# Two transformer blocks on one core: low parts of the weights by accumulating DMAs in the first feed-forward

## The chip, the cores and the metric

The kernel runs on one core of one Trainium2 chip. The metric is the device time of one execution in microseconds. A core has TensorE (PE, matmuls into PSUM), VectorE (DVE), ScalarE (ACT), GpSimd (POOL) and SyncE (SP); SP, ACT and POOL issue DMAs. Each engine works through its own queue in order, and they are tied together by semaphores.

## The reference

Two hybrid transformer blocks follow each other on 16 meta tokens and 512 tokens of width 1024, in float32. The first mixes a short convolution, retention and differential attention and ends in a feed-forward; the second mixes stick-breaking attention and gated linear attention and has a gated feed-forward. What the change touches is the feed-forward of the first block:

```
D_MODEL = 1024
D_FF = 4 * D_MODEL
...
    x = x + merged @ w_out

    u = jnp.square(jax.nn.relu(rms_norm(x, norm2_w) @ w_up))
    return x + u @ w_down
```

## The kernel before

**Products in three passes.** All activations lie with their features on the 128 partitions and the tokens along the free axis. Every product with a weight is done as three products of rounded operands: a float32 value is split into a high part, rounded to the matmul's type `fp32r`, and a low part, the difference. A product is high x high, high weight x low activation, and low weight x high activation. The high and low parts of the activations lie in `xh`, `xl` and `bh`, `bl`.

**Strips.** The weights come from HBM as 331 strips of 128 x 8 x 128 values (512 KB), 128 output columns each. There are two buffers for the raw strip (`wraw`), for its high part (`wh`) and for its low part (`wl`), used in turn: `slot` is the strip's number modulo 2. For a strip n:

- SP loads it (`load`, L366) when the low part of strip n-2 is made (`lo_done`), which is the last reader of that raw buffer.
- ACT rounds it: `split_hi` (L401 to L406) waits for the load and until strip n-2 is multiplied (`mm_done`), and writes `wh`, which counts `hi_done`.
- DVE subtracts: `split_lo` (L972 to L976) waits for `hi_done` and writes `wl = wraw - wh`, which counts `lo_done`.
- PE multiplies: `strip` (L1776 to L1801) waits for `hi_done` and for the eviction of strip n-2, does 8 matmuls of the pass high x high and 8 of high x low, waits for `lo_done`, and does 8 of low x high; the last one counts `mm_done`. A strip with `ready` (the first of each phase whose input is being made) instead waits for `lo_done` at once and goes by chunks of the input, three matmuls each.

**The first feed-forward.** Its 4096 hidden features are done in four groups of 1024. A group is 8 up strips (`ffn0up` to `ffn3up`, source `bh`, `bl`) and 8 down strips (`ffn0down` to `ffn3down`, source `xh`, `xl`), 64 strips in all, for 512 tokens.

- In an up strip n, ACT (`up_strips`, L663 to L673) first does `split_hi` of strip n+1, waits for the matmuls of n, writes relu of the sum to `tmp` (L671), waits for DVE's `u_scaled`, and rounds the result to `xh` (`hi_of`, L414). DVE (L1341 to L1359) does, through `begin` (L978), `split_lo` of strip n+1 and waits for the matmuls of n; it then squares by relu(sum) x `tmp` (L1348, which frees the PSUM bank), multiplies by the norm's row `rsq` (L1354), and makes `xl` after `xh` (L985).
- In a down strip, ACT only does `split_hi` (`splits`, L487). DVE's `accumulate` (L1324 to L1331) does `begin` and adds the sum to `res`. The last down group goes through `finished_rows` instead, with norms of the next block in between.
- GpSimd has loaded the attention tables before (L2429) and built the masks (L2431 to L2447); its next work is a loop of subtractions for gated linear attention (L2450 on), much later.

The order on each queue is the program's order: what stands in the loop body is what each engine does next.

Of the kernel before, what the change touches and what calls it, by code (L numbers as in the profile page):

```python
# [23 lines left out]
ALU = mybir.AluOpType  # L24
ACT = mybir.ActivationFunctionType
# [4 lines left out]
KC = D // P  # L30
# [37 lines left out]
START = {}  # L68
# [47 lines left out]
def build(nc, weights, cols, tables, consts, lam_rows, post_rows, x_t, meta2_t, wgk, gla_masks, res_dram,  # L116
          mrg_dram, out):
    ctx = ExitStack()
    with ctx:
# [3 lines left out]
        def sem(name):  # L123
            return ctx.enter_context(nc.semaphore(name))
# [89 lines left out]

        w_loaded = [sem("w_loaded0"), sem("w_loaded1")]
        hi_done, lo_done = sem("hi_done"), sem("lo_done")
        mm_done = sem("mm_done")
        evicted = [sem("evicted0"), sem("evicted1")]
        in_ready, op_ready = sem("in_ready"), sem("op_ready")
# [171 lines left out]
        def _(act):  # L391
# [9 lines left out]
            def split_hi(n, half, slot):  # L401

                act.wait_ge(w_loaded[slot], 16 * half + 16)
                if not (isinstance(n, int) and n < 2):
                    act.wait_ge(mm_done, n - 1)
                nc.scalar.activation(wh[:, slot], wraw[:, slot], ACT.Copy).then_inc(hi_done, 1)  # L406

            def begin(n_half_slot, next_one):

# [77 lines left out]
            def splits(B, count):  # L487

                with act.Fori(0, count // 2) as i:
                    for j in range(2):  # L490
                        split_hi(*pos(B, j + 1, i))
# [168 lines left out]
            for g in range(4):  # L660
                B = START[f"ffn{g}up"]

                def up_strips(i):  # L663
                    for j in range(2):
                        p0, p1 = pos(B, j, i), pos(B, j + 1, i)
                        split_hi(*p1)
                        if g == 0 and isinstance(i, int) and j == 0:
                            act.wait_ge(sums_done, 2)
                            root(rsq[:, NM:T], ps[:, 4, :], 1.0 / D, -1.0)
                        act.wait_ge(mm_done, p0[0] + 1)  # L670
                        nc.scalar.activation(tmp[:, j, NM:T], slot_ap(p0[2], SEQ), ACT.Relu).then_inc(relu_ready, 1)  # L671
                        act.wait_ge(u_scaled, KC * g + 2 * i + j + 1)
                        hi_of(flat(xh[:, bass.ds(2 * i + j, 1), NM:T]), hf[:, j, NM:T])  # L673

                first_then_loop(act, KC // 2, up_strips)
                n_hi += KC
                if g < 3:
                    splits(START[f"ffn{g}down"], KC)
                if g == 2:
                    act.wait_ge(meta_in, 16)  # L680
                    nc.scalar.activation(msq.rearrange("p (c t) -> p c t", c=KC), res[:, :, 0:NM], ACT.Square)
                    act.wait_ge(meta_scaled, 1)
                    nc.scalar.activation(bh[:, :, 0:NM], mscaled.rearrange("p (c t) -> p c t", c=KC), ACT.Copy)\
                        .then_inc(meta_hi, 1)
# [282 lines left out]
        def _(dve):  # L967
# [4 lines left out]
            def split_lo(n, half, slot):  # L972

                dve.wait_ge(hi_done, n + 1)
                nc.vector.tensor_tensor(wl[:, slot], wraw[:, slot], wh[:, slot].bitcast(F32), ALU.subtract)\  # L975
                    .then_inc(lo_done, 1)  # L976

            def begin(this, next_one):  # L978
                split_lo(*next_one)
                dve.wait_ge(mm_done, this[0] + 1)  # L980

            def lo_of(dst, src, hi, ready, n):
# [341 lines left out]
            def accumulate(B, n=SEQ):  # L1324

                with dve.Fori(0, KC // 2) as i:
                    for j in range(2):
                        p0 = pos(B, j, i)
                        begin(p0, pos(B, j + 1, i))
                        r = flat(res[:, bass.ds(2 * i + j, 1), T - n:T])  # L1330
                        nc.vector.tensor_tensor(r, slot_ap(p0[2], n), r, ALU.add).then_inc(evicted[p0[2]], 1)  # L1331

# [5 lines left out]
            for g in range(4):  # L1338
                B = START[f"ffn{g}up"]

                def up_strips(i):  # L1341
                    for j in range(2):
                        p0 = pos(B, j, i)
                        begin(p0, pos(B, j + 1, i))
                        dve.wait_ge(relu_ready, KC * g + 2 * i + j + 1)
                        dve.wait_ge(op_ready, (3 + g) * KC + 2 * i + j - 1)

                        nc.vector.scalar_tensor_tensor(out=hf[:, j, NM:T], in0=slot_ap(p0[2], SEQ), scalar=0.0,  # L1348
                                                       in1=tmp[:, j, NM:T], op0=ALU.max, op1=ALU.mult)\
                            .then_inc(evicted[p0[2]], 1)  # L1350
                        if g == 0 and isinstance(i, int) and j == 0:
                            root_made()
                        dve.wait_ge(evicted[p0[2]], p0[1] + 1)
                        nc.vector.tensor_tensor(hf[:, j, NM:T], hf[:, j, NM:T], rsq[:, NM:T], ALU.mult)\  # L1354
                            .then_inc(u_scaled, 1)
                        dve.wait_ge(u_scaled, KC * g + 2 * i + j + 1)
                        c = bass.ds(2 * i + j, 1)
                        lo_of(flat(xl[:, c, NM:T]), hf[:, j, NM:T], flat(xh[:, c, NM:T]), op_ready,
                              n_hi + 2 * i + j + 1)  # L1359

                first_then_loop(dve, KC // 2, up_strips)
                n_hi += KC
                if g < 3:
                    accumulate(START[f"ffn{g}down"])
                if g == 2:
                    dve.wait_ge(meta_in, 16)
                    m3 = mscaled.rearrange("p (c t) -> p c t", c=KC)
                    nc.vector.tensor_tensor(m3, res[:, :, 0:NM],
                                            wcols("norm_mix_pre_2").unsqueeze(2).to_broadcast([P, KC, NM]), ALU.mult)\
                        .then_inc(meta_scaled, 1)  # L1370
                    dve.wait_ge(meta_hi, 1)
                    link(nc.vector.tensor_tensor(bl[:, :, 0:NM], m3, bh[:, :, 0:NM].bitcast(F32), ALU.subtract))
# [1045 lines left out]
        @block.gpsimd  # L2418
        def _(pool):
            for h in range(RH + DH):  # L2420
                if h == 0:
                    pool.wait_ge(op_ready, KC)
                elif h == RH:
                    pool.wait_ge(op_ready, 2 * KC)
                elif 1 < h < RH:
                    pool.wait_ge(rs_masked, 5 * (h - 1))
                elif h > RH + 1:
                    pool.wait_ge(ds_ready, 3 * (h - RH - 1))
                pool.dma_start(tbl[h % 2], tables[h]).then_inc(table_in[h % 2], 16)  # L2429

            nc.gpsimd.memset(sbmask[:], 0.0).then_inc(pool_self, 1)  # L2431

            def masked_where(lo, hi, base, step, per_partition, op):

                masked_where.n += 1
                pool.wait_ge(pool_self, masked_where.n)
                m = sbmask[:, lo:hi]
                nc.gpsimd.affine_select(out=m, in_=m, compare_op=op, fill=-1e30, base=base, pattern=[[step, hi - lo]],
                                        channel_multiplier=per_partition).then_inc(pool_self, 1)

            masked_where.n = 0
            for lo, hi, base in ((0, P, 0), (272, 400, 0), (416, 432, 112), (432, 448, 0)):
                masked_where(lo, hi, base, 1, -1, ALU.is_gt)
            masked_where(416, 432, -111, 0, 1, ALU.is_gt)
            pool.wait_ge(const_in, 16)
            pool.wait_ge(pool_self, 6)
            nc.gpsimd.tensor_copy(identb[:], ident).then_inc(masks_made, 1)  # L2447


            for h in range(GH):  # L2450
                pool.wait_ge(gcum_done, 2 * h + 1)
                for k, L, lo in levels():
                    m = 7 * h + k
                    if m >= 2:
                        pool.wait_ge(gx_ready, m - 1)
                    d, s_ = halves(grow[m % 2], L, lo), halves(cums[h % 2], L, lo)
                    n = (T - lo) // (2 * L)
                    mid = s_[:, :, 0, L - 1:L].to_broadcast([P, n, L])
                    nc.gpsimd.tensor_tensor(d[:, :, 0, :], mid, s_[:, :, 0, :], ALU.subtract)
                    nc.gpsimd.tensor_tensor(d[:, :, 1, :], s_[:, :, 1, :], mid, ALU.subtract).then_inc(gd_ready, 1)  # L2460
# [130 lines left out]
```

## Time and profile before

| | us |
|---|---|
| median of three runs | 2198.74 (2198.53 to 2198.84) |
| span of the profiled execution | 2196.6 |
| PE busy | 2150.5 (98%) |
| DVE busy | 1150.0 (52%) |
| ACT busy | 776.6 (35%) |
| POOL busy | 51.3 (2%) |

How to read it: busy times are added up by engine; a share of the span is a mean over stages with different limits. Times of instructions are counted from the start of the profiled span. Where several instructions of one kind follow each other, a line shows them together with their count. "L1797" is a line of the kernel's file; that of a helper stands for all its callers, and the names of tiles tell them apart. Matmuls overlap, so their durations are longer than their distance.

### The profile page before, as it was taken

The page shows a single profiled execution, that of the slowest core. Times are in us where ns is not written, and L with a number is a line of the kernel's source. Part 1 is how long each engine was busy: PE and PEld are TensorE (multiplying, and loading weights), DVE is VectorE, ACT ScalarE, POOL GpSimd, SP SyncE. Part 2 cuts the span into 40 slices and gives each one's busy share as a digit, 9 for nine tenths or more (in the row PEclk, how much of TensorE's full clock was granted, in tenths as well). Part 3 has the DMA queues.
Part 4 walks back from the last instruction along what each step waited for, and adds up shares of the span by engine and source line. Part 5 has one row for each costly group of instructions (what it writes and reads, how often), then busy time and mean ns, then how long its engine had stood idle before and what let it go on. Part 6 is the DMA issues. An engine that isn't in the chain of part 4 may idle for free.

```text
span 2196.6 us, 33725 instructions
## 1 busy us (share of the span) xinstructions
PE 2150.5 (98%) x13184; PEld 1851.5 (84%) x13184; DVE 1150.0 (52%) x1719; ACT 776.6 (35%) x1214; POOL 51.3 (2%) x79
## 2 busy tenths in 40 slices
PE   9999998999999999999999999999999989999998
PEld 8988994677888778888888888999999988889896
DVE  6553332443555645535445665457755556546365
ACT  4222221332344533323223466333433333222233
POOL 0000000000000000000000000012200000000000
PEclk9999999999999999999999999999999999999999
DMA  4232220132222132223222221231123222222222
GB/s 148 93 105 95 86 86 20 58 106 95 74 72 68 58 126 96 92 96 101 90 96 95 83 92 58 86 118 59 54 103 128 94 77 77 95 87 96 96 87 96
DMA packets 52966, 194.66 MB, mean 89 GB/s; under 512 B 6896, under 2 KB 7280, under 8 KB 52224
## 3 DMA queue, kind: packets, MB, share of 16 engines
q1 hardware_dynamic: 49248, 177.56, 24.6%
q10 hardware_dynamic: 2656, 12.41, 1.5%
q0 software_dynamic: 960, 3.24, 0.5%
q8 instruction: 75, 1.23, 0.2%
q14 instruction: 27, 0.22, 0.0%
HBM read 186.77 MB, written 6.42 MB: 88 GB/s over the span
## 4 chain that ended last, share of the span: by engine, by line
PE 93%; DVE 4%; ACT 2%; issue 1%; DMA 0%; DVEq 0%; ACTq 0%; SPq 0%
PE ps L1797 75%; PE ps L2356 5%; PE ps L2223 1%; PE ps L2013 1%; PE ps L2038 1%; PE ps L1972 1%; PE ps L1957 1%; PE ps L2288 1%; PE ps L2129 1%; DVE kk_r L1441 1%; PE ps L2052 1%; ACT kk L715 0%; ACT kk L716 0%; PE ps L2266 0%; PE ps L2110 0%
## 5 line engine op out<-in xcount | busy, mean ns | idle before, releaser
L406 ACT ACTIVATE wh<-wraw 128x1024 fp32r<-128x1024 f32 x330 | 348.2, 1055 | 834.4 <-PE ps L1797 725.5
L975 DVE TENSOR_TENSOR wl<-wraw,wh 128x1024 fp32r<-128x1024 f32 x330 | 403.4, 1223 | 144.9 <-ACT wh L406 138.0
L1797 PE MATMUL ps<-xh,wh 128*128 128x264 f32 (+1 forms) x2088 | 392.2, 333 | 9.7 <-ACT wh L406 5.7
L1797 PE MATMUL ps<-xh,wl 128*128 128x264 f32 (+1 forms) x2088 | 385.9, 330 | 0.0
L1797 PE MATMUL ps<-xl,wh 128*128 128x264 f32 (+1 forms) x2088 | 385.8, 330 | 0.0
L1797 PEld LDWEIGHTS ps<-xh,wh 128*128 128x128 f32 x2088 | 315.9, 189 | 51.8 <-ACT wh L406 4.6
L1797 PEld LDWEIGHTS ps<-xh,wl 128*128 128x128 f32 x2088 | 316.3, 188 | 38.2
L1797 PEld LDWEIGHTS ps<-xl,wh 128*128 128x128 f32 x2088 | 316.3, 188 | 38.2
L1797 PE MATMUL ps<-bh,wh 128*128 128x264 f32 (+1 forms) x1296 | 234.3, 325 | 3.9 <-DVE hf L1008 1.7
L1797 PE MATMUL ps<-bl,wh 128*128 128x264 f32 (+1 forms) x1296 | 230.9, 322 | 0.0
L1797 PE MATMUL ps<-bh,wl 128*128 128x264 f32 (+1 forms) x1296 | 230.6, 322 | 0.0
L1797 PEld LDWEIGHTS ps<-bh,wh 128*128 128x128 f32 x1296 | 191.4, 188 | 27.1 <-DVE hf L1008 2.2
L1797 PEld LDWEIGHTS ps<-bl,wh 128*128 128x128 f32 x1296 | 191.3, 188 | 19.8 <-issue 0.2
L1797 PEld LDWEIGHTS ps<-bh,wl 128*128 128x128 f32 x1296 | 191.0, 188 | 19.6
L1008 DVE TENSOR_TENSOR qq<-ps,rsq 128x528 f32<-128x528 f32 (+2 forms) x36 | 25.3, 704 | 80.6 <-PE ps L1797 80.5
L414 ACT ACTIVATE bh<-hf 128x512 f32 (+1 forms) x38 | 24.0, 632 | 103.3 <-DVE hf L1697 52.3
L1008 DVE TENSOR_TENSOR tmp<-ps,rsq 128x528 f32<-128x528 f32 x31 | 21.9, 708 | 64.9 <-PE ps L1797 63.3
L1331 DVE TENSOR_TENSOR res<-ps,res 128x512 f32 x24 | 16.6, 692 | 72.5 <-PE ps L1797 72.5
L2356 PE MATMUL ps<-wh,bh 128*128 128x512 f32 x176 | 49.1, 393 | 0.0
L2356 PE MATMUL ps<-wh,bl 128*128 128x512 f32 x176 | 49.0, 393 | 0.0
L2356 PE MATMUL ps<-wl,bh 128*128 128x512 f32 x176 | 49.0, 393 | 0.0
L1008 DVE TENSOR_TENSOR gate<-ps,rsq 128x512 f32<-128x512 f32 (+1 forms) x24 | 16.7, 697 | 57.8 <-PE ps L1797 56.3
(420 smaller groups left out, 2030.1 us busy)
## 6 DMA issues: line engine op xcount, KB each, us to landing
wraw<-weights_dram SPq DMA_DIRECT2D x331, 512.0 KB, 3.5
hf<-tables_dram POOLq DMA_DIRECT2D x12, 264.0 KB, 3.0
res<-x_t_dram SPq DMA_DIRECT2D x4, 528.0 KB, 7.4
res<-x_t_dram ACTq DMA_DIRECT2D x1, 2112.0 KB, 9.1
res_dram<-res ACTq DMA_DIRECT2D x1, 2112.0 KB, 7.7
mrg_dram<-mrg ACTq DMA_DIRECT2D x1, 2112.0 KB, 7.3
mrg<-mrg_dram ACTq DMA_DIRECT2D x1, 2112.0 KB, 10.6
res<-res_dram ACTq DMA_DIRECT2D x1, 2112.0 KB, 16.5
```

The source lines that it names most:

```text
L406: nc.scalar.activation(wh[:, slot], wraw[:, slot], ACT.Copy).then_inc(hi_done, 1)
L414: nc.scalar.activation(dst, src, ACT.Copy, scale=scale).then_inc(hf_hi, 1)
L975: nc.vector.tensor_tensor(wl[:, slot], wraw[:, slot], wh[:, slot].bitcast(F32), ALU.subtract)\
L1008: return nc.vector.tensor_tensor(dst, src, row(rsq, n), ALU.mult)
L1441: ins = nc.vector.tensor_tensor(dst, src, hi.bitcast(F32), ALU.subtract)
L1797: last = nc.tensor.matmul(o, w[:, slot, c, :], a[:, c, tok], start=(k == 0), stop=(k == len(steps) - 1))
L1957: ins = nc.tensor.matmul(o, keys, qq[:, h, NM + q0:T], start=True, stop=True)
L1972: ins = nc.tensor.matmul(o, vt[:, t, f:f + P], at[:, t - 1, q0:SEQ], start=False, stop=(t == 4))
L2013: ins = nc.tensor.matmul(ps[:, 2 + m, off:off + W], dq[h % 2][f, NM + P * b:NM + P * b + P], dk[h % 2][f, 0:W], start=True, stop=True)
L2038: nc.tensor.matmul(ps[:, 6, q0:SEQ], vt[:, t, P * h:P * h + P], at[:, t, q0:SEQ], start=(t == 0), stop=False)
L2052: nc.tensor.transpose(ps[:, 4, P * k:P * k + P], a[:, keys:keys + P], ident)
L2356: last = nc.tensor.matmul(ps[:, 2 * t + h, :], a[:, c, NM + P * t:NM + P * t + P], w[:, slot, 4 * h:4 * h + 4, :].rearrange("p k n -> p (k ...
```

## The change

ACT, after it has rounded a strip to `wh`, writes the negative of the same rounding to `wl` (`split_minus_hi`) and counts `minus_hi`. GpSimd waits for each of these and issues a DMA from SBUF to SBUF that adds the raw strip onto `wl`, so that `wl = wraw - wh` stands there when it has landed; a semaphore for each slot counts it (`raw_added`). DVE no longer subtracts: `begin_added` waits for the landing of the next strip's DMA and counts `lo_done` by a nop, in the place where the subtraction stood. This is done for 56 strips in a row, from the second up strip of the first group to the first down strip of the last group. The first up strip of the first group and the last seven down strips keep the subtraction, as does all the rest of the kernel. SP's loads, PE's waits and the buffers stay as they are.

```diff
@@ -214,6 +214,7 @@
         w_loaded = [sem("w_loaded0"), sem("w_loaded1")]
         hi_done, lo_done = sem("hi_done"), sem("lo_done")
+        minus_hi, raw_added = sem("minus_hi"), [sem("raw_added0"), sem("raw_added1")]
         mm_done = sem("mm_done")
@@ -404,6 +405,11 @@
                 nc.scalar.activation(wh[:, slot], wraw[:, slot], ACT.Copy).then_inc(hi_done, 1)
+
+            def split_minus_hi(n, half, slot):
+
+                split_hi(n, half, slot)
+                nc.scalar.activation(wl[:, slot], wraw[:, slot], ACT.Copy, scale=-1.0).then_inc(minus_hi, 1)
 
@@ -663,7 +669,7 @@
                         p0, p1 = pos(B, j, i), pos(B, j + 1, i)
-                        split_hi(*p1)
+                        split_minus_hi(*p1)
@@ -675,7 +681,9 @@
                 if g < 3:
-                    splits(START[f"ffn{g}down"], KC)
+                    with act.Fori(0, KC // 2) as i:
+                        for j in range(2):
+                            split_minus_hi(*pos(START[f"ffn{g}down"], j + 1, i))
@@ -979,6 +987,15 @@
+            def begin_added(this, next_one):
+
+                _, half, slot = next_one
+                first = START["ffn0up"] + 1
+                done = half - (first + (slot != first % 2)) // 2 + 1
+                dve.wait_ge(raw_added[slot], 16 * done)
+                nc.vector.nop().then_inc(lo_done, 1)
+                dve.wait_ge(mm_done, this[0] + 1)
+
@@ -1326,7 +1343,7 @@
                         p0 = pos(B, j, i)
-                        begin(p0, pos(B, j + 1, i))
+                        begin_added(p0, pos(B, j + 1, i))
                         r = flat(res[:, bass.ds(2 * i + j, 1), T - n:T])
@@ -1341,7 +1358,7 @@
                         p0 = pos(B, j, i)
-                        begin(p0, pos(B, j + 1, i))
+                        begin_added(p0, pos(B, j + 1, i))
                         dve.wait_ge(relu_ready, KC * g + 2 * i + j + 1)
@@ -2446,6 +2463,12 @@
             nc.gpsimd.tensor_copy(identb[:], ident).then_inc(masks_made, 1)
 
+            first = START["ffn0up"] + 1
+            for k in range(56):
+                slot = (first + k) % 2
+                pool.wait_ge(minus_hi, k + 1)
+                pool.dma_start(wl[:, slot], wraw[:, slot], accum_op=ALU.add).then_inc(raw_added[slot], 16)
+
```

## Rows read from the trace of the kernel before

**Rows 1.** The page: busy time, share of the span and instructions of each engine.

```profile
PE 2150.5 (98%) x13184; PEld 1851.5 (84%) x13184; DVE 1150.0 (52%) x1719; ACT 776.6 (35%) x1214; POOL 51.3 (2%) x79
```

**Rows 2.** By stretches (us), TensorE alone: length, busy, granted clock, DMA share, GB/s.

```profile
892.00:1205.00 313.00, 313.00 (x1351) 1.00 0.29 94
...
1800.00:2196.00 396.00, 381.13 (x2148) 0.99 0.27 88
```

**Rows 3.** The chain that ended last, its piece in this stage: start, length, what.

```profile
892.74 317.46 PE ps L1797 x1370
```

**Rows 4.** In order of time: start, us, engine, line, operation; one up strip.

```profile
921.79 2.01 PE L1797 MATMUL ps<-bh,wh 128*128 128x512 f32 x8
...
922.71 0.69 DVE L1348 SCALAR_TENSOR_TENSOR hf<-ps,tmp 128x512 f32<-128x512 f32 x1 [1.16 <-ACT tmp L671]
923.44 0.69 DVE L1354 TENSOR_TENSOR hf<-hf,rsq 128x512 f32<-128x512 f32 x1
...
924.26 0.63 ACT L414 ACTIVATE xh<-hf 128x512 f32 x1 [1.67 <-DVE hf L1354]
924.80 1.04 ACT L406 ACTIVATE wh<-wraw 128x1024 fp32r<-128x1024 f32 x1
...
925.88 1.23 DVE L975 TENSOR_TENSOR wl<-wraw,wh 128x1024 fp32r<-128x1024 f32 x1
...
927.27 19.80 SPq L366 DMA_DIRECT2D wraw<-weights_dram  x5
927.35 2.01 PE L1797 MATMUL ps<-bh,wh 128*128 128x512 f32 x8
927.55 0.60 ACT L671 ACTIVATE tmp<-ps 128x512 f32<-128x512 f32 x1 [1.71 <-PE ps L1797]
928.27 0.69 DVE L1348 SCALAR_TENSOR_TENSOR hf<-ps,tmp 128x512 f32<-128x512 f32 x1 [1.17 <-ACT tmp L671]
```

**Rows 5.** Durations (ns, min/median/max) of both split lines, 890 to 1160 us.

```profile
L406 ACT ACTIVATE wh<-wraw x49: 1042/1049/1062, 890.4 to 1156.8; 128x1024 fp32r<-128x1024 f32 x49
...
L975 DVE TENSOR_TENSOR wl<-wraw,wh x49: 1224/1226/1227, 891.5 to 1158.0; 128x1024 fp32r<-128x1024 f32 x49
```

**Rows 6.** In order of time: two activations of ScalarE, one right behind the other.

```profile
882.24 1.06 ACT L406 ACTIVATE wh<-wraw 128x1024 fp32r<-128x1024 f32 x1 [3.37 <-PE ps L1797]
...
883.20 0.71 ACT L414 ACTIVATE bh<-res,col 128x512 fp32r<-128x512 f32 x1
```

**Rows 7.** The stage as one stretch: length, busy of PE, PEld, DVE, ACT, POOL; clock, DMA.

```profile
891.80:1204.00 312.20, 312.20 (x1347) 252.78 (x1346) 151.85 (x179) 96.95 (x124) 0.00 (x0) 1.00 0.29 94
```

**Rows 8.** In order of time: GpSimd's last mask and its next instruction.

```profile
710.59 0.55 POOL L2447 CAST identb<-cst 128x128 bf16<-128x128 f32 x1
1465.41 0.61 POOL L2459 TENSOR_TENSOR res<-res 128x256 f32<-128x256 f32 x1 [754.27 <-DVE res L1527]
```

**Rows 9.** The page, DMA issues: count, KB each, median us from issue to landing.

```profile
wraw<-weights_dram SPq DMA_DIRECT2D x331, 512.0 KB, 3.5
hf<-tables_dram POOLq DMA_DIRECT2D x12, 264.0 KB, 3.0
...
out_dram<-qq SPq DMA_DIRECT2D x7, 256.0 KB, 2.1
```

**Rows 10.** The page, DMA queues: packets, MB, share of 16 engines' span.

```profile
q1 hardware_dynamic: 49248, 177.56, 24.6%
...
q0 software_dynamic: 960, 3.24, 0.5%
```

**Rows 11.** Groups of eight strips as stretches (columns of rows 7), the second and third.

```profile
936.40:980.80 44.40, 44.40 (x193) 36.02 (x192) 17.04 (x18) 9.05 (x9) 0.00 (x0) 1.00 0.29 95
980.80:1025.30 44.50, 44.50 (x194) 36.10 (x193) 24.61 (x31) 16.79 (x24) 0.00 (x0) 1.00 0.29 94
```

**Rows 12.** In order of time: the first up strip of the first group begins.

```profile
887.54 0.40 PE L1797 MATMUL ps<-bh,wh 128*128 128x512 f32 x1
...
890.40 1.06 ACT L406 ACTIVATE wh<-wraw 128x1024 fp32r<-128x1024 f32 x1 [0.69 <-issue]
```

**Rows 13.** In order of time: a down strip on ScalarE and VectorE.

```profile
944.25 1.06 ACT L406 ACTIVATE wh<-wraw 128x1024 fp32r<-128x1024 f32 x1 [4.50 <-PE ps L1797]
944.38 0.69 DVE L1331 TENSOR_TENSOR res<-ps,res 128x512 f32 x1 [3.38 <-PE ps L1797]
945.35 1.23 DVE L975 TENSOR_TENSOR wl<-wraw,wh 128x1024 fp32r<-128x1024 f32 x1 [0.27 <-ACT wh L406]
```

**Rows 14.** The raw strips' loads, 900 to 1300 us: issue to landing.

```profile
DMA to landing us min/median/max: 3.2/3.4/4.5
```

**Rows 15.** By stretches (columns of rows 2): the end of the kernel.

```profile
2185.00:2190.00 5.00, 1.47 (x7) 1.00 0.55 203
2190.00:2196.00 6.00, 0.00 (x0) 0.54 0.47 175
```

## The prediction, made before the changed kernel was run

> **What bounds the kernel now.** I read the page first, then the stage of the first feed-forward by stretches, then the chain that ended last, and then one strip in order of time on every engine. The page gives TensorE 98% of the span, VectorE 52%, ScalarE 35% and GpSimd 2% [rows 1]. In the stretch from 892 to 1205 us TensorE is busy for 313.00 of 313.00 us, at a granted clock of 1.00, which is its upper level of 2.4 GHz [rows 2]. The chain that ended last runs through this stage in one piece of 317.46 us that is nothing but the matmuls of L1797 [rows 3]. So there is no idle time of TensorE here to be won back, and whatever is taken off VectorE in this stage is worth nothing by itself. The only question is whether something new becomes longer than TensorE's time for a strip.
>
> That time is the step from 921.79 to 927.35, 5.56 us for 24 matmuls [rows 4]; the stage has 64 such strips, and the change touches the low parts of 56 of them (1 to 56, counted from the first strip of ffn0up as 0).
>
> **The loop of an up strip, before.** The same rows show a loop beside TensorE, for a strip n: VectorE evicts n (L1348 at 922.71), scales it (923.44), ScalarE rounds it to xh (924.26) and then makes wh of strip n+2 (924.80), VectorE makes wl of n+2 (925.88, done 927.11), and only then may it evict n+1. Both queues are in order, so the eviction stands behind the weight's low part. From one eviction to the following wh is 924.80 - 922.71 = 2.09 us; from there to the end of wl 2.31 us. The loop takes about 4.5 us against 5.56, so it has 1.1 us to spare. This is the margin that the change spends.
>
> **Removed.** 56 subtractions of 1.226 us are 68.7 us of VectorE [rows 5]. TensorE waits for none of them: worth 0 us.
>
> **Added on ScalarE.** 56 negated roundings of the same shape as wh, 1.05 us each [rows 5], stand behind wh; a 128x1024 activation followed by another one is 0.96 us from start to start (882.24 to 883.20) [rows 6]. So the negated strip is complete 0.96 + 1.05 = 2.01 us after wh begins. The 59 us themselves fit, as ScalarE is busy for 96.95 of 312.20 us in this stage [rows 7]; what counts is where the 1.05 us lies, in the loop.
>
> **Added on GpSimd and the DMA queues.** GpSimd waits for minus_hi and issues a 512 KB accumulating transfer from SBUF to SBUF. Behind these waits on its queue stand only the subtractions of the later attention, which begin at 1465 us [rows 8]; they lose nothing. A queue takes about 0.16 us from the event to the issue, as SP does from wl (done 927.11) to its load (927.27) [rows 4]. No row shows an accumulating transfer, so I bound its time X from issue to landing. Lower end: GpSimd's plain 264 KB transfer lands in 3.0 us [rows 9]; its queue used 0.5% of 16 engines' span [rows 10], so 0.005 x 16 x 2196.6 / 12 / 16 = 0.92 us on each engine for one transfer, hence 1.77 us for 512 KB, and a plain 512 KB would land in 3.0 + 0.85 = 3.85 us. An accumulation must also read its destination: another 1.77 us gives 5.6 us, which I take, since reading twice is the least that adding needs. Upper end: the whole plain transfer twice, 7.7 us; I keep 9 us for the range, since nothing bounds the adding itself. The quickest large transfer of the whole trace, 256 KB from SBUF, takes 2.1 us [rows 9].
>
> The Trainium skill, "DMA: Bandwidth & Descriptors", section "Anatomy of one DMA", fits a transfer from GpSimd with 2.0 us plus its bytes at 436 GB/s, an estimate of 3.2 us for 512 KB; by it the sum below would end at about 2259 us. The trace's own 264 KB transfer, 3.0 us where this fit gives 2.6, speaks against so low a value, and the fit was made on plain copies.
>
> **The new wait.** begin_added makes VectorE wait for the landing of n+1 before it evicts n, with the operand's scaling and low part queued behind; ScalarE's xh waits for these, and wh and the negated copy of n+2 stand behind xh. So the DMA lies in the loop: 2.09 (eviction to wh) + 2.01 + 0.16 + X + 0.20 (landing to eviction with the nop between; I take 0.12 from the end of relu at 928.15 to the eviction at 928.27 [rows 4], and 0.08 for the nop) = 4.46 + X. With X = 5.6 an up strip takes 10.06 us in place of 5.56. TensorE's third pass waits for the low part, and nothing hides that.
>
> A whole group from the start of its first up strip: wh of the second strip begins at 0.2, its low part lands at 2.37 + X = 7.97, and the low part of the first down strip seven rounds later, at 7.97 + 7 x 10.06 = 78.4 us. That strip waits for it before its first matmul. Before, it began after 8 x 5.56 = 44.5 us, which the stretches of about 44.5 us show as always filled with 192 to 194 matmuls [rows 11]. The group loses 33.9 us (8X - 10.9), four groups **135.6 us**. In the first group wh of the second strip begins at 890.40 and not 0.2 us after the strip's start at 887.54, because ScalarE is busy before it [rows 12]: 2.7 us more, less 0.9 us that the norm's sums cost there already, **1.8 us**.
>
> **The down strips.** Here ScalarE and VectorE have no loop between them: wh begins 0.2 us after a strip starts, and wl starts 1.1 us later (944.25, 945.35) [rows 13]. A low part lands at 0.2 + 2.01 + 0.16 + X after its predecessor started, 7.97, and is needed at 5.56 + 16 matmuls = 9.27: covered by 1.3 us. The other loop is the buffer of the raw strip: wh and its negation 2.01, issue 0.16, X, SP's issue 0.16, the load 3.4 [rows 14], 0.15 to the next wh: 5.88 + X = 11.48 per two strips against 11.12. Followed strip by strip over the eight: the second waits 0.8 us (its wh stands behind the last xh), then every second one 0.3, and the next up group begins its loop 1.65 us later: 3.5 us a group, three groups **10.4 us**. Loads and accumulations now run at once in this stage, where DMA engines were 29% busy; the slowest load of the stage took 4.5 us against 3.4 [rows 14]. I allow **5 us**, between 0 and 24 x 0.55 = 13. The last down group keeps VectorE's subtractions.
>
> Sum: 135.6 + 1.8 + 10.4 + 5 = 152.8 us. On the profiled execution, 2196.6 us, this is 2349.4; the median of the runs, 2198.74, lies 2.1 above that span, so I predict 2352 us.
>
> **The rivals.**
> The first: a cheap accumulation, which overlaps its two reads, X = 3.85. Then 4 x (30.8 - 10.9) + 1.8 = 81 us and covered down strips, 2280 us. For it speaks how little of the DMA engines is used (29%); against it the extra read. Chance 0.17 for X below 4.5; 0.03 of it for a transfer much below 3.85, as one would be whose fixed part is that of the 2.1 us store: at X = 3.2, with the same formula, 4 x 14.7 + 1.8 = 61 us and 2259 us. The Trainium skill's fit named above is this case.
> The second: an expensive accumulation, X = 7.7 to 9: groups of 50.7 to 61.1 us, 205 to 246 in all, down strips at 6.8 to 7.4 us, 38 to 55 more, 2445 to 2500 us. For it: no row of this trace has an adding transfer; its arithmetic may set its pace. Chance 0.28, of which 0.10 lie beyond 2500.
> The third: TensorE's clock. It now pauses about 1.5 and 3.0 us in each up strip. The trace shows the granted clock at 1.00 in the stretch in which TensorE stops at the end and at a mean of 0.54 in the following one, with no matmul [rows 15]: it does go to 1.2 GHz after a pause. If it did so here a strip would take up to 2 x 5.56 = 11.1 us, 1 us more than the new loop, 33 us in all: 2385 us. In the stretch from 1800 to 2196 with its many short pauses the clock stays at 0.99 [rows 2], against it. Chance 0.07, inside the range.
> The fourth, on the other side: the transfer is hidden. It decides at X = 5.56 - 4.46 = 1.1 us: below that the loop stays shorter than TensorE's strip and the time is 2199 us, not faster, as TensorE has no gap here. The quickest transfer of half the size takes 2.1 us. It would also be so if the transfer were waited for elsewhere than ahead of the eviction, but the diff puts it there. Chance 0.03, the case included that the transfer is not what releases the wait.
>
> **How the numbers follow.** The likeliest case (X from 4.5 to 7.5) has 0.45, with the clock's 0.07 beside it. The range from 2280 to 2500 leaves out about 0.05 below (the fourth rival and the lowest part of the first) and 0.10 above. A measurement of this kernel tells about 0.2%, 4.4 us, from no change. Slower by more has 0.97, within 0.02, faster 0.01.
>
> **What would show it.** In the changed kernel: TensorE idle once or twice in each up strip, and VectorE's eviction there (L1348 now) waiting for the DMA and no longer for relu; a period near 10 us there and below 6.5 us in the down strips; TensorE's third pass the one that waits; 56 issues on GpSimd with a landing near 5.6 us, and the up period minus this landing near 4.5 us. If the period stays at 5.56 with landings above 2 us, my loop is wrong; if the landing is far from 5.6, only a size is.

## The result, and the profile after

The changed kernel takes 2348.24 us (three runs, 2343.35 to 2350.75) against 2198.74 before: a ratio of 1.0677, 95% interval 1.0658 to 1.0696. The profiled execution is the one of 2343.35 us, span 2341.6; before, the span was 2196.6, so there are 145.0 us to account for.

From the page of the changed kernel: the busy times of the engines, GpSimd's DMA queue, and the new transfers' row of issues (count, KB each, median us from issue to landing).

```profile
PE 2189.1 (93%) x13184; PEld 1859.5 (79%) x13184; DVE 1081.6 (46%) x1663; ACT 826.6 (35%) x1270; POOL 99.8 (4%) x135
...
q0 software_dynamic: 9024, 32.61, 7.2%
...
wl<-wraw POOLq DMA_DIRECT2D x56, 512.0 KB, 4.6
```

VectorE has lost 68.4 us of work against [rows 1] and TensorE, which does the same matmuls, is busy for 93% of a longer span. What VectorE saved was worth nothing; the time went into waiting. Who waited for whom in the stage (us in total, times, longest), in the changed kernel:

```profile
DVE hf L1365 <- DMA wl<-wraw: 201.1, 32, 7.3
ACT xh L420 <- DVE hf L1371: 196.5, 32, 6.5
DVE res L1348 <- DMA wl<-wraw: 139.8, 24, 7.7
PEld ps L1814 <- DVEq L996: 101.0, 43, 7.7
ACT wh L407 <- DMA wraw<-weights_dram: 84.6, 15, 6.9
```

All 32 evictions of up strips (L1365, before L1348) now wait for the transfer, and behind each of them ScalarE waits for VectorE. L996 is the nop that counts `lo_done`. The fifth row is the other loop, that of the raw strip's buffer: ScalarE waits for raw strips in the down groups and at their ends, which it did nowhere in this stage before.

One up strip in order of time, the counterpart of [rows 4]:

```profile
925.23 0.69 DVE L1365 SCALAR_TENSOR_TENSOR hf<-ps,tmp 128x512 f32<-128x512 f32 x1 [6.28 <-DMA wl<-wraw]
925.95 0.69 DVE L1371 TENSOR_TENSOR hf<-hf,rsq 128x512 f32<-128x512 f32 x1
926.78 0.63 ACT L420 ACTIVATE xh<-hf 128x512 f32 x1 [6.32 <-DVE hf L1371]
927.32 1.04 ACT L407 ACTIVATE wh<-wraw 128x1024 fp32r<-128x1024 f32 x1
...
928.27 1.04 ACT L412 ACTIVATE wl<-wraw 128x1024 fp32r<-128x1024 f32 x1
928.41 2.13 PE L1814 MATMUL ps<-bh,wh 128*128 128x512 f32 x8 [1.38 <-ACT wh L407]
...
929.60 0.85 POOL L2470 DMA_DIRECT2D wl<-wraw  x1 [8.47 <-ACT wl L412]
...
934.22 3.25 PE L1814 MATMUL ps<-bh,wl 128*128 128x512 f32 x8 [1.83 <-DVEq L996]
934.52 0.69 DVE L1365 SCALAR_TENSOR_TENSOR hf<-ps,tmp 128x512 f32<-128x512 f32 x1 [6.25 <-DMA wl<-wraw]
```

The loop can be read off from one eviction to the next: 2.09 us to wh (927.32), 1.99 to the end of the negated copy (929.31), 0.29 to GpSimd's issue (929.60), 4.55 to the landing, 0.37 to the next eviction: 9.29 us. TensorE, which has 5.56 us of work, pauses twice in it, 1.38 us for wh and 1.83 us for the low part, and some of its matmuls are slow (the eight of 934.22 take 3.25 us where such eight take 2.0 to 2.1).

The groups, by TensorE's first matmul in each. The lines with xh are the first strips of down groups, those with bh the first strips of up groups; the stage begins at 887.5, as before, and its last down group ends at 1389.5.

```profile
962.16 0.79 PE L1814 MATMUL ps<-xh,wh 128*128 128x512 f32 x1 [7.23 <-DVEq L996]
...
1015.85 2.01 PE L1814 MATMUL ps<-bh,wh 128*128 128x512 f32 x8
...
1092.04 0.79 PE L1814 MATMUL ps<-xh,wh 128*128 128x512 f32 x1 [7.20 <-DVEq L996]
...
1141.57 2.02 PE L1814 MATMUL ps<-bh,wh 128*128 128x512 f32 x8
...
1216.63 0.79 PE L1814 MATMUL ps<-xh,wh 128*128 128x512 f32 x1 [6.06 <-DVEq L996]
...
1265.19 2.01 PE L1814 MATMUL ps<-bh,wh 128*128 128x512 f32 x8
...
1342.49 0.79 PE L1814 MATMUL ps<-xh,wh 128*128 128x512 f32 x1 [6.42 <-DVEq L996]
```

| | before, us each | after, us | lost |
|---|---|---|---|
| four up groups | 45.4, then 44.5 | 74.7, 76.2, 75.1, 77.3 | 124.4 |
| three down groups | 44.5 | 53.7, 49.5, 48.6 | 18.3 |
| last down group | 44.5 | 47.0 | 2.5 |

So the up groups hold six sevenths of the loss, and every down group begins with a pause of 6 to 7 us. But not all that is lost in an up group comes from its own loop. The first transfer issued in a group should land 7.05 us after the group's start (0.2 + 2.01 + 0.29 + 4.55). In the first group it lands 9.8 us after it, which the prediction's 2.7 us for that group explain. In the other three it lands after 11.0, 10.2 and 12.3 us, as the engines come late out of the down group before: 12.3 us in all.

### The profile page after: what moved, and what is told of

Its sections match the earlier page's. It is cut to its first block, busy times and chain, and to the rows that moved or that the text cites. A ratio compares the mean times of both kernels' runs of the same rounds, so it can differ in the third digit from the quotient of the medians.

```text
span 2341.6 us, 33836 instructions
## 1 busy us (share of the span) xinstructions
PE 2189.1 (93%) x13184; PEld 1859.5 (79%) x13184; DVE 1081.6 (46%) x1663; ACT 826.6 (35%) x1270; POOL 99.8 (4%) x135
## 4 chain that ended last, share of the span: by engine, by line
PE 75%; DMA 12%; ACT 5%; DVE 5%; issue 3%; ACTq 0%; DVEq 0%; SPq 0%
PE ps L1814 58%; DMA wl<-wraw 9%; PE ps L2373 5%; DMA wraw<-weights_dram 2%; ACT wl L412 2%; ACT wh L407 1%; PE ps L2240 1%; PE ps L2030 1%; DVE hf L1371 1%; DVE hf L1365 1%; PE ps L2055 1%; PE ps L1989 1%; PE ps L1974 1%; PE ps L2305 1%; PE ps L2146 1%
## 5 line engine op out<-in xcount | busy, mean ns | idle before, releaser
L983 DVE TENSOR_TENSOR wl<-wraw,wh 128x1024 fp32r<-128x1024 f32 x274 | 334.7, 1223 | 134.3 <-ACT wh L407 129.7
L1814 PE MATMUL ps<-bh,wl 128*128 128x264 f32 (+1 forms) x1296 | 243.3, 333 | 45.3 <-DVEq L996 45.3
L1814 PE MATMUL ps<-bh,wh 128*128 128x264 f32 (+1 forms) x1296 | 240.1, 329 | 28.7 <-ACT wh L407 24.3
L1814 PEld LDWEIGHTS ps<-bh,wl 128*128 128x128 f32 x1296 | 194.2, 192 | 76.2 <-DVEq L996 57.3
L1365 DVE SCALAR_TENSOR_TENSOR hf<-ps,tmp 128x512 f32<-128x512 f32 x32 | 22.1, 692 | 201.1 <-DMA wl<-wraw 201.1
L420 ACT ACTIVATE xh<-hf 128x512 f32 (+1 forms) x32 | 20.2, 630 | 196.5 <-DVE hf L1371 196.5
L1348 DVE TENSOR_TENSOR res<-ps,res 128x512 f32 x24 | 16.6, 692 | 139.8 <-DMA wl<-wraw 139.8
L2470 POOL DMA_DIRECT2D wl<-wraw x56 | 48.3, 863 | 579.2 <-ACT wl L412 579.2
L412 ACT ACTIVATE wl<-wraw 128x1024 fp32r<-128x1024 f32 x56 | 58.4, 1042 | 0.0
## 6 DMA issues: line engine op xcount, KB each, us to landing
mrg<-mrg_dram ACTq DMA_DIRECT2D x1, 2112.0 KB, 10.7
```

Source lines behind the costliest of these rows:

```text
L412: nc.scalar.activation(wl[:, slot], wraw[:, slot], ACT.Copy, scale=-1.0).then_inc(minus_hi, 1)
L420: nc.scalar.activation(dst, src, ACT.Copy, scale=scale).then_inc(hf_hi, 1)
L1814: last = nc.tensor.matmul(o, w[:, slot, c, :], a[:, c, tok], start=(k == 0), stop=(k == len(steps) - 1))
L2470: pool.dma_start(wl[:, slot], wraw[:, slot], accum_op=ALU.add).then_inc(raw_added[slot], 16)
```

## The experiments

My theory after the result: two loops. In the up groups the transfer stands in the loop through VectorE and ScalarE (about 4.75 us plus the landing). In the down groups the raw buffer's loop sets the pace, with transfers and loads that slow each other. The rivals: that the low part is simply too late for TensorE wherever it is awaited; that it is the traffic, or the accumulating itself, that costs; that a lower clock of TensorE costs.

**One kind of group at a time.** The transfers only in the up groups (the down groups' evictions go back to `begin` with its subtraction):

```diff
-                    with act.Fori(0, KC // 2) as i:
-                        for j in range(2):
-                            split_minus_hi(*pos(START[f"ffn{g}down"], j + 1, i))
+                    splits(START[f"ffn{g}down"], KC)
...
-            for k in range(56):
+            for k in range(32):
```

> Only the 32 low parts that are made during the four up groups come by accumulating transfer; the 24 that are made during down groups are subtracted on VectorE as before. My theory: the up groups lose what they lose in the changed kernel, 8 x 9.30 - 44.5 and so 26 to 29 us each, and the down groups only the slow first matmuls: 110 to 120 us in all, about 2315 us. A rival that puts the loss into the transfers' traffic, in proportion to their number, gives 32/56 of 150, 85 us, 2284 us.

Measured: 2319.78 us, ratio 1.0549 (1.0531 to 1.0566), 121 us more than before, and by the evictions an up strip of 9.3 us and a down strip of 5.56. The up groups take 74.6, 72.3, 72.0 and 73.2 us, 113.3 more than before. In the four down groups no transfer is made, and they lose 8.3 us. The second of them as a stretch (length, busy of PE, PEld, DVE, ACT, POOL with counts, granted clock, DMA share, GB/s):

```profile
1082.13:1128.70 46.57, 46.57 (x192) 37.66 (x193) 16.71 (x18) 9.00 (x9) 0.00 (x0) 0.95 0.31 102
```

TensorE never waits in it; its 192 matmuls take 2.1 us more at a mean granted clock of 0.95. That is what the clock costs at a group's start. The other half, the transfers only in the down groups (`split_hi` in `up_strips`, 24 transfers):

> Only the 24 low parts that are made during the three down groups come by accumulating transfer, the 32 of the up groups are subtracted on VectorE. My theory: no loop through VectorE and ScalarE there, only the raw buffer's loop with an overlapped transfer; a down strip takes 5.8 to 7.1 us in place of 5.56, 6 to 37 us in all, about 2220 us. If the loss went with the number of transfers, 24/56 of 150 would be 64 us, 2263 us.

Measured: 2207.78 us, ratio 1.0038 (1.0024 to 1.0052), 9 us. A loss in proportion to the number of transfers is excluded: 3.8 us for each of 32, 0.4 us for each of 24. But the halves add up to 130 us and not to 149: in the changed kernel the down groups and the late starts behind them cost 18.3 + 12.3 = 30.6 us, and the down groups alone 9. The chain of this half alone shows how the loop of the raw buffer runs there (start, us, what):

```profile
951.03 4.54 DMA wl<-wraw
955.79 4.80 DMA wraw<-weights_dram
963.00 4.56 DMA wl<-wraw
```

Here the two slots bunch: the accumulation of the other slot starts at 954.21, 3.2 us behind the first, lands after 5.2 us, and their loads follow as closely. In the changed kernel, which enters the group out of the up strips' slow loop, the slots alternate, each accumulation beside the other slot's load:

```profile
978.18 7.18 DMA wl<-wraw
985.58 4.35 DMA wraw<-weights_dram
992.34 7.15 DMA wl<-wraw
999.71 4.49 DMA wraw<-weights_dram
```

That is 14.2 us for two strips in the first down group (978.18 to 992.34), against 12.0 us bunched (951.03 to 963.00; the pairs before and behind it take 11.6 and 11.3). Its second and third down groups begin in the one pattern and go over to the other, and they are the shorter ones. The three runs of the changed kernel spread over 7 us, those of the kernel before over 0.3; that the two patterns cause this was not tried.

**The wait taken out of VectorE's queue.** SyncE, which needs the landing anyway before it reloads the raw buffer, waits for it and counts:

```diff
             def begin_added(this, next_one):
...
-                dve.wait_ge(raw_added[slot], 16 * done)
-                nc.vector.nop().then_inc(lo_done, 1)
                 dve.wait_ge(mm_done, this[0] + 1)
...
+            def added(i, k):
+                n, slot = 2 * i + k, k
+                sp.wait_ge(raw_added[k], 16 * (i - 65 + k))
+                nc.sync.nop().then_inc(lo_done, 1)
+                load(n, slot)
```

> The changed kernel, with one thing moved: VectorE no longer waits for the transfer's landing ahead of its eviction. SyncE, which has to wait for the same landing before it reloads the raw buffer, waits for it and counts lo_done. My theory (the wait in VectorE's queue closes the loop eviction, xh, wh, negated copy, transfer, eviction): the loop is open, an up strip goes from 9.30 us to between 5.6 us and 7.1 us, the bounds of the raw buffer's loop (2.01 + 0.29 + transfer + 0.1 + load + 0.15, with 4.55 and 3.4 us alone, 7.2 and 4.4 us where load and transfer overlap, for two strips). Over 56 strips that is 2200 to 2285 us, and I expect about 2230 us. The rival (the transfer is too late for TensorE's third pass wherever it is awaited): up strips stay near 9.3 us and the time near 2340 us.

Measured: 2270.0 us, ratio 1.032 (1.0303 to 1.0337). An up strip falls from 9.3 us to 6.4 to 7.1 (mean of each group), so the loop was the cause of most; but 71 us remain and not the 31 of the expectation. Something else was open.

**Small loads.** The changed kernel with loads of one chunk of eight for the strips that follow in the accumulated buffers, so its products are of other weights:

```diff
+            def added(i, k):
+                n, slot = 2 * i + k, k
+                sp.wait_ge(lo_done, 2 * i + k - 1)
+                sp.dma_start(wraw[:, slot, 0:1], weights[bass.ds(n, 1), :, 0:1].rearrange("a p k n -> p (a k) n"))\
+                        .then_inc(w_loaded[slot], 16)
```

> The changed kernel, but the loads of the 56 strips whose buffers the accumulations read bring only one of eight chunks (64 KB for 512 KB); the rest of a raw strip stays old, so the products are of other weights. My theory (an accumulation takes 4.55 us alone and 7.2 us because a load of 512 KB runs beside it): in the down groups the accumulation falls to 4.6 to 4.9 us and a strip to 5.56 us, in the up groups nothing changes (9.30 us); some 25 to 30 us are saved, about 2320 us. The rival (accumulations are slow there because TensorE and the engines are busier, or because they meet each other): down strips stay at 6 to 7 us and the time near 2345 us.

Measured: 2322.76 us, one run. The accumulations land in 4.5 us (median of all 56), down strips take 5.6 to 5.7 us on the mean, up strips still 9.3. The small loads themselves land in 1.9 us and not in 3.5, so the raw buffer's loop is shorter twice over. By its sum the shorter load alone should not matter: with 3.5 us and an undisturbed accumulation two strips need 2.01 + 0.29 + 4.55 + 0.2 + 3.5 + 0.15 = 10.7 us, less than TensorE's 11.1. So I put the 25 us down to the contention, as expected; this run does not separate the two. Both edits together:

> Both edits together: SyncE waits for the landing in VectorE's place, and the 56 loads are of 64 KB each (products of other weights). If the loop through VectorE and the overlap of load and accumulation are the whole of the loss, nothing of it is left: 2199 to 2204 us, with TensorE without gaps at 5.56 us a strip. If the accumulating transfers cost something else (a slower TensorE, a lower clock, a slower ScalarE), it shows here as a time above 2210 us.

Measured: 2235.52 us, ratio 1.0165 (1.0148 to 1.0182), at least 31 us above the 2199 to 2204 expected: the two loops are not the whole of it. TensorE in that kernel, at the start of its first down group:

```profile
941.28 0.79 PE L1832 MATMUL ps<-xh,wh 128*128 128x512 f32 x1 [3.99 <-SPq L382]
941.87 0.63 PE L1832 MATMUL ps<-xl,wh 128*128 128x512 f32 x1
942.30 0.63 PE L1832 MATMUL ps<-xh,wl 128*128 128x512 f32 x1
...
946.99 0.46 PE L1832 MATMUL ps<-xl,wh 128*128 128x512 f32 x1
947.28 0.39 PE L1832 MATMUL ps<-xh,wl 128*128 128x512 f32 x1
947.51 0.39 PE L1832 MATMUL ps<-xh,wh 128*128 128x512 f32 x1
```

The first strip of a down group wants its low part before its first matmul, because it goes by chunks of its input. It waits 3.99 us, and its next matmuls are 0.43 us apart and not 0.23: TensorE runs at the lower of its two levels after the pause, for 6 us (the mean granted clock from 941 to 950 us is 0.66). Up strips take 5.9 us. Two more kernels, built on this one, test this account. The first lets that strip do its 16 matmuls with the high part first:

```diff
-                pe.wait_ge(lo_done if ready is not None else hi_done, number + 1)
+                pe.wait_ge(lo_done if ready is not None and not late else hi_done, number + 1)
...
+                if late:
+                    steps = [(c, *p) for c in chunks for p in passes[:2]] + [(c, *passes[2]) for c in chunks]
```

> The kernel with the landing awaited by SyncE and the thin loads (products of other weights), 2235.5 us, with one thing more: the first strip of a down group does its 16 matmuls with the weight's high part first and waits for the low part only then, as all other strips do. My theory of the 36 us that were left there: in each of the four groups that strip waits 4.0 us for the low part before its first matmul and does its first matmuls at 0.43 us instead of 0.23 (2.5 us more), 26 us in all; the rest, 11 us, is an up strip at 5.9 us, whose low part lands 9.9 us after its predecessor began, 0.6 later than its third pass. Then this kernel takes about 2210 us. If the 36 us are the transfers' own cost on TensorE, it stays at 2235.

Measured: 2212.11 us, ratio 1.0063 (1.0046 to 1.0079), where 2210 was expected. The second also leaves out the negated copy, so its low parts are other numbers too:

> The kernel before this one, and the negated copy left out as well (thin loads, and low parts of other numbers): the transfer starts 0.95 us earlier. The low part of an up strip then lands 9.0 us after its predecessor began and is needed at 9.27, so all strips take 5.56 us. Nothing of the loss is left, 2199 to 2203 us, although the 56 accumulating transfers still run. If more than 2206 us is measured, a part of the loss is not explained.

Measured: 2202.42 us, ratio 1.0018 (1.0008 to 1.0027). The stage in that kernel as a stretch, columns as above:

```profile
892.00:1205.00 313.00, 310.52 (x1335) 250.24 (x1334) 82.28 (x121) 95.84 (x122) 48.23 (x56) 1.00 0.53 105
```

TensorE is busy for 310.52 of 313 us at a clock of 1.00 while all 56 transfers run. Of 149.5 us all but 3.6 are now named, and 2.5 of these are four waits of TensorE for the last chunk of xl, which the new order of the matmuls wants earlier. The same reordering with full loads and the reference's numbers:

> A whole kernel with full loads and the reference's numbers: SyncE waits for the landing instead of VectorE, and the first strip of a down group asks for the low part only at its third pass. The kernel with the first of these edits took 2270.0 us. By the same account the second saves up to 26 us, about 2248 us; what is left is the overlap of loads and accumulations in the raw buffer's loop. If that loop alone sets the pace, the time gained at a group's start is lost again within the group and it stays near 2268.

Measured: 2261.38 us (2252.29 to 2264.32), ratio 1.0271 (1.0249 to 1.0293): between the two expectations. Part of what the group's start gives is taken back by the raw buffer's loop: in its first two down groups a strip takes 6.5 to 7.4 us, where the kernel with the first edit alone has 5.5 to 7.3. None of these beats the kernel before.

**What the adding costs.** Plain copies in place of the accumulating ones, so the low part is a copy of the weight:

```diff
-                pool.dma_start(wl[:, slot], wraw[:, slot], accum_op=ALU.add).then_inc(raw_added[slot], 16)
+                pool.dma_start(wl[:, slot], wraw[:, slot]).then_inc(raw_added[slot], 16)
```

> The changed kernel with plain copies in place of the accumulating ones: the same 512 KB, the same queue, nothing is added (the low part becomes a copy of the weight, so the result is of other numbers). It measures what the adding costs. By the sum of the prediction a plain transfer lands in 3.85 us; the accumulating one takes 4.55 alone. Then an up strip falls from 9.30 to 8.60 us, 22 us in all, and with shorter down strips the time is about 2315 us. If the adding is free, the landing stays at 4.5 us and the time at 2345; if the two reads are carried one after the other, the plain copy is below 3.3 us and the time below 2300.

Measured: 2271.43 us, one run, below the 2300 that I had named for a copy landing in less than 3.3 us, and not the 2315 expected. GpSimd's transfers, up group and then down group, first of the changed kernel:

```profile
L2470 POOL DMA_DIRECT2D wl<-wraw x8: 852/857/919, 892.7 to 957.5; - x8
...
DMA to landing us min/median/max: 4.5/4.6/4.6
...
L2470 POOL DMA_DIRECT2D wl<-wraw x8: 862/862/862, 966.8 to 1013.6; - x8
DMA to landing us min/median/max: 4.6/7.2/7.8
```

and of the kernel with plain copies:

```profile
L2470 POOL DMA_DIRECT2D wl<-wraw x9: 527/527/557, 894.2 to 955.2; - x9
DMA to landing us min/median/max: 2.9/2.9/2.9
...
L2470 POOL DMA_DIRECT2D wl<-wraw x9: 527/527/530, 967.0 to 1016.0; - x9
DMA to landing us min/median/max: 2.9/2.9/3.5
```

The plain copy lands in 2.9 us, and the accumulating one in 4.55, so the adding costs 1.65 us alone. GpSimd's queue is taken for 0.33 us longer by it (0.86 against 0.53). In the down groups the plain copy mostly stays at 2.9 us (3.5 at most), where the accumulating one goes to 7.2. This does not show that adding is what makes the transfer sensitive to a load beside it: in the down groups of this kernel a copy runs beside a load for only 0.9 to 1.6 us, while in the changed kernel's first down group an accumulation has a load beside it for 4.4. A plain copy with a whole load beside it was not tried. An up strip takes 7.68 us here: less its landing, 4.77, the same constant as in the changed kernel (9.32 less 4.55).

**A link of the loop.** Without the negated copy, so GpSimd's transfer adds onto what stands in `wl`:

```diff
-                nc.scalar.activation(wl[:, slot], wraw[:, slot], ACT.Copy, scale=-1.0).then_inc(minus_hi, 1)
...
-                pool.wait_ge(minus_hi, k + 1)
+                pool.wait_ge(hi_done, first + k + 1)
```

> The changed kernel without the negated copies on ScalarE: GpSimd issues its transfer when wh is made, and it accumulates onto what stands in wl (so the low parts are of other numbers). My theory (the negated copy is a link of the loop, 0.95 us from start to start): an up strip takes 8.35 us in place of 9.30, 29 us less, and the raw buffer's loop is shorter by 0.95 us for two down strips: together about 2310 us. If ScalarE's copy were beside the loop, the time would stay near 2345 us.

Measured: 2302.93 us, one run. Two evictions of that kernel in order of time:

```profile
930.50 0.69 DVE L1364 SCALAR_TENSOR_TENSOR hf<-ps,tmp 128x512 f32<-128x512 f32 x1 [5.31 <-DMA wl<-wraw]
...
938.85 0.69 DVE L1364 SCALAR_TENSOR_TENSOR hf<-ps,tmp 128x512 f32<-128x512 f32 x1 [5.31 <-DMA wl<-wraw]
```

8.35 us, as expected to the hundredth.

**The traffic without its waits.** The kernel before, with 52 transfers of the same form between buffers that rest in this stage:

```diff
+            pool.wait_ge(lo_done, first + 1)
+            for k in range(52):
+                pool.wait_ge(hi_done, first + k + 1)
+                if k >= 2:
+                    pool.wait_ge(raw_added[k % 2], 16 * (k // 2))
+                pool.dma_start(vt[:, 1 + k % 2, :], flat(qq)[:, D * (k % 2):D * (k % 2) + D], accum_op=ALU.add)\
+                    .then_inc(raw_added[k % 2], 16)
```

> The kernel before, all subtractions on VectorE, and beside them 52 accumulating transfers of 512 KB from GpSimd between two buffers that nobody uses in this stage; no engine of the stage waits for them. The same traffic without its waits. My theory (the loss is waiting, not traffic): the loads go from 3.4 to about 4.4 us and the accumulations to about 7 us, all of it hidden, and the time stays within 3 us of 2199 us. The rival (traffic slows the engines or the loads so far that TensorE waits): above 2210 us.

Measured: 2198.39 us, ratio 0.9998 (0.9989 to 1.0008). The stage as a stretch, columns as above:

```profile
892.00:1205.00 313.00, 313.00 (x1351) 253.42 (x1350) 152.24 (x179) 97.57 (x125) 44.77 (x52) 1.00 0.81 182
```

DMA engines 81% busy where they were 29% [rows 2], and not one pause of TensorE. The landings are not those expected: a load starts 1.1 us behind an accumulation here, and they land in 5.6 and 5.5 us (medians; 8.5 and 9.4 at most), hidden. In the changed kernel's first down group the load starts 0.3 us behind, and they land in 4.4 and 7.2. The traffic is free; the waits are the whole loss.

## Why the prediction was right, and where its terms were off

- **TensorE bounds the stage, VectorE's work is worth nothing.** Right: 68 us of VectorE fewer, and no stretch of the stage became shorter.
- **The loop.** Right, and shown by moving its wait, by taking out one link (0.95 us) and by a shorter transfer (1.65 us). Its constant was 4.46 and measured about 4.75: GpSimd issues 0.29 us after the negated copy, where I took SyncE's 0.16, and from landing to eviction pass 0.37, where I took 0.20 (0.08 of it a guess for the nop, which no row showed).
- **The transfer.** 5.6 predicted, 4.55 measured. The mis-sized part is the plain copy: 3.85 predicted, 2.9 measured. I had scaled GpSimd's load from HBM [rows 9]; the copy inside SBUF of twice the size lands sooner than that load. The term for the adding was sized well, 1.77 against 1.65; that it is a second read, as I argued, no run shows. The Trainium skill's 3.2 us ("DMA: Bandwidth & Descriptors", "Anatomy of one DMA") is near the plain copy and 1.35 us below the accumulating one.
- **The up groups.** The same working with the measured sizes gives 0.2 + 2.01 + 0.29 + 4.55 + 7 x 9.30 - 44.5 = 27.65 us a group, with the first group's 1.8 together 112.4. Measured: 113.3 in the kernel with transfers in the up groups alone, and 124.4 less the late starts' 12.3, 112.1, in the changed kernel. With my sizes it was 137.4. This term was 25 us too high.
- **The down groups.** 10.4, the late start of the next up group among it, plus 5 for contention predicted; measured 18.3 in the groups and 12.3 in the late starts, 30.6. Here a step failed, not only a size. I bounded contention by the slowest load of the trace, 4.5 us; most loads of the down groups stayed there (the slowest of the stage took 5.8), but the accumulation, for which I allowed nothing, went from 4.55 to 7.2 and once to 8.0. And I followed the slots strip by strip from the state in which the kernel before leaves the up group. Alone this gives the right size (9 us measured); behind slow up groups the slots alternate and the loop takes 14.2 us for two strips, not 11.5. In this pattern a strip takes about 7.1 us, above the 6.5 that I had named as a sign.
- **The errors cancel, and the number is in part luck.** 25 us too much and 15 too little; with the 2.5 us of the last group, for which I had nothing, the sum was 152.8 for 145.0 in the profiled execution. My working as it stands, with the measured landing of 4.55 us put in, gives 4 x 25.5 + 1.8 = 103.8 us for the up groups and covered down strips, about 2303 us: 46 us below the median. The landing also lies at the very edge between my likeliest case (from 4.5 us) and the first rival. So the loop was right, and the time within 4 us was not earned.
- **The first matmul of a down group.** I used it in the working (the group ends with the landing of the next group's first low part) but did not see that it stands by itself: with VectorE free of the wait it still costs 4.0 us and a slow start, four times, and up strips keep a second path, over TensorE's third pass, of 5.9 us. The diff's one visible wait was not the only one.
- **The rival of the clock.** It had 0.07 and came in part. The pause before the changed kernel's first down group and the 3.8 us behind it, as stretches:

```profile
958.00:962.20 4.20, 0.04 (x1) 0.04 (x1) 0.00 (x0) 0.00 (x0) 0.36 (x1) 0.59 0.66 125
962.20:966.00 3.80, 3.80 (x10) 3.03 (x11) 2.08 (x3) 2.00 (x3) 0.00 (x0) 0.55 0.39 138
```

  Around the pause of 7.23 us the mean granted clock falls to 0.59 and 0.55, near the lower level, and the strip behind it takes 7.2 us (962.16 to 969.39) and not 5.6. Over the four groups this is 1.6 to 2.6 us each, about 8 us, as the 8.3 us of the down groups without transfers. In the up strips, where I had placed it, slow matmuls come too (the 3.25 us of 934.22 for eight), but the period there stays at 9.3 us: they are hidden by the waits. The Trainium skill, "TensorE: Matmul & The Clock Gate", section "Part 1: The HAM clock gate (the "warmup" mystery)", describes these two levels; the trace agrees, with 0.43 and 0.23 us a matmul.
- **The side.** The other side needed a transfer of 1.1 us, and even a plain copy took 2.9.

## What to carry to other kernels

Before work is moved off an engine that is not the bound, write down the loop that its queue closes and what it has to spare; here it had 1.1 us, and even the plain copy took 2.9. A wait for a transfer belongs to the engine that has nothing else queued behind it, and even then every reader of the result has a deadline of its own. An accumulating transfer is sized alone and beside the loads that will run with it, and a sum that comes out right is still to be checked term by term.

## What the runs showed of the hardware that I had not expected

- An accumulating transfer of 512 KB inside SBUF lands in 4.55 us alone and in 7.2 us with a 512 KB load that starts 0.3 us behind it; the load itself goes from 3.5 to 4.4 us. The plain copy lands in 2.9 us, and in 2.9 to 3.5 us with 0.9 to 1.6 us of a load beside it.
- Where the load starts 1.1 us behind the accumulation, in other buffers and with nobody waiting for the accumulations, they land in 5.6 and 5.5 us, and TensorE never pauses. Which of the two differences matters was not tried.
- GpSimd's issue of an accumulating transfer takes 0.86 us of its queue, of a plain one 0.53.
- A raw strip's loop of two slots has two patterns at the same work, bunched (11.3 to 12.0 us for two strips) and alternating (14.2 us).
